# A two-block transformer forward pass on one core: norm statistics by token, eight slots of split weights, a first group of four units and a spare PSUM bank

## The chip, the core and the metric

The kernel runs on one core of a Trainium2 chip. Its engines are TensorE (PE in the rows), VectorE (DVE), ScalarE (ACT), GpSimd (POOL) and SyncE (SP). The metric is the device time of one execution in microseconds (us); the time of the kernel before is the median of three runs.

## The reference

Two blocks are computed one after the other on x of 512 tokens by 1024 features, in float32. Everything between the norms is a chain of products of an activation and a weight matrix:

```python
# first block: gmlp layer, feed-forward, banded attention layer, feed-forward
h = h + rms_norm(m, g[1])                       # m: gmlp or attention branch
f = jnp.square(jax.nn.relu(rms_norm(h, g[2]) @ w_up)) @ w_down
h = h + rms_norm(f, g[3])
# second block
h = h + 0.5 * swiglu(rms_norm_2(h, ffn1_norm), w_gate, w_up, w_down)
z = rms_norm_2(h, mix_norm) @ w_in              # top-k attention, retention, gates (rope by positions)
h = h + merged @ w_out
h = h + 0.5 * swiglu(rms_norm_2(h, ffn2_norm), ...)
h = h + sigmoid(rms_norm_2(h, ple_norm) @ w_ple_gate) * (p @ w_ple_proj)
return rms_norm_2(h, final_norm)
```

rms_norm divides by the root of the mean square of a token (plus 1e-6) and multiplies by a gain per feature.

## The kernel before

Activations lie feature-major: eight tiles of 128 features by 512 tokens (`DT` = 8). Precision comes from splitting: a value is written as a high part in the type float32r and a low part (the rest), and each product of a weight tile and an activation tile is three matmuls, high by high, high by low, low by high (`three_passes`, L368 to L370). Activations in split form are XH and XL, or HH and HL for the hidden layer.

The weights come as 411 **units**, numbered in the order in which TensorE uses them. A unit is 128 x 1024 float32 (some are narrower) and makes one PSUM bank of 128 x 512 from eight tiles, so from 24 matmuls. A unit is loaded by SP into RAW (4 slots), its high part is written to WH and its low part to WL (4 slots each): by ACT (`split_high`, L797) and DVE (`split_low`, L1128) in their instruction streams, just behind the work on the unit four places earlier, or by POOL (L316 and L319) in the ranges of `POOL_RANGES`. Those are units 0 to 19, 92 to 119 and 256 to 326. The semaphores count in unit order, so the first DVE split behind a POOL range waits until POOL has finished its last unit (`weights_split`), and the first ACT split likewise (`high_split`).

TensorE makes unit u in bank u mod 4 once its split is there and the unit before it in that bank is evacuated by DVE. Stages and their first units: gmlp_v 0, gmlp_u 8, gmlp_out 16, ffn_a0 24, att_v 88, att_kq 96, att_out 112, ffn_a1 120, ffn_b1 184, mix_heads 252, ret_qk 263, ret_v 271, ret_gate 279, merge 287, mix_out 319, ffn_b2 327, ple 395. A feed-forward takes groups: 8 units up (16 in the gated ones), then 8 units down, whose sums DVE adds into M; M is cleared by a memset at the start (L1229).

At a boundary between a branch and the next stage this happens. DVE copies the last bank into M, ACT squares it, DVE adds it to SS (`branch`, L1182 and L1140). `stat` (L460) multiplies SS by a matrix of ones, which gives each token's sum on all partitions; ACT takes the root into RI (L836), DVE the reciprocal of 128 x 512 (L1158). `post_and_pre` then goes over the eight tiles: z = M x RI (L1169), H updated (L1170), ACT squares H and writes XH, DVE writes XL (L1148). TensorE works on the first three units of the stage together, tile by tile as XL comes (`together`), with the second `stat` ahead of their last tile; the RI of that second norm is needed before the units can be evacuated (L1202, L1211). For token-major products `stat` also makes the sums with tokens on the partitions (L458, four matmuls of one column), and RT holds their reciprocal.

The rotation tables (sine and cosine, `rotation_tables`) are made on DVE and ACT during the last eight units of ffn_a1.

## Time and profile before

| | us |
|---|---|
| median of 3 runs (2697.91 to 2699.78) | 2698.27 |
| the profiled execution, its own time | 2702.41 |
| its span | 2700.6 |
| TensorE busy | 2487.4 |
| VectorE busy | 1434.4 |
| ScalarE busy | 796.1 |
| GpSimd busy | 518.7 |
| mean granted TensorE clock | 0.944 of full |

Matmuls are pipelined, so the busy time of TensorE counts overlaps as one; its idle time is what the boundaries between stages cost, and the clock column of a stretch shows whether its matmuls ran at 2.4 GHz (1.00) or at 1.2 GHz (0.50). DVE, ACT and POOL are busy for about half of the span or less, so they matter only where TensorE waits for one of them.

### The profile page before, as it was taken

To read this page: it belongs to the slowest core of one execution; us is meant where nothing else is said; L and a number is where in the kernel's file an instruction comes from. 1 tells how busy PE (TensorE), PEld (TensorE's weight loads), DVE (VectorE), ACT (ScalarE), POOL (GpSimd) and SP (SyncE) were. 2 spreads that over 40 slices of the span, in tenths; PEclk is the share of its full clock that TensorE was granted. 3 is DMA by queue.
4 is the path that set the end of the run, shared out by engine and by line. 5 is a ranking of instruction groups with operands and counts; after the bars stand their busy time and mean duration, and the time that the engine had idled before them with its cause. 6 is when DMAs were issued, how large, how long until landed. Compare 5 with 4: busy or idle time off the path is not lost.

```text
span 2700.6 us, 30486 instructions
## 1 busy us (share of the span) xinstructions
PE 2487.4 (92%) x10766; PEld 1964.8 (73%) x10766; DVE 1434.4 (53%) x1974; ACT 796.1 (29%) x1226; POOL 518.7 (19%) x243
## 2 busy tenths in 40 slices
PE   6888999979998999996999997978989998999996
PEld 5666888856666788884888885555567887888875
DVE  4566434473666543457534466797434336444456
ACT  2134223331433332233323232312322113322233
POOL 6600000015432000000000005452026871000000
PEclk9889999989998999997999998986599999999998
DMA  4222333322222233321333332121012323333322
GB/s 165 70 78 63 94 101 94 93 71 85 84 62 63 86 94 100 94 82 55 109 95 100 95 88 75 48 77 32 0 43 74 100 87 94 101 96 99 88 76 70
DMA packets 64805, 221.52 MB, mean 82 GB/s; under 512 B 7504, under 2 KB 9680, under 8 KB 64592
## 3 DMA queue, kind: packets, MB, share of 16 engines
q1 hardware_dynamic: 59184, 208.17, 26.0%
q10 hardware_dynamic: 5536, 12.19, 1.4%
q8 instruction: 56, 0.92, 0.1%
q14 instruction: 29, 0.24, 0.0%
HBM read 218.23 MB, written 2.10 MB: 82 GB/s over the span
## 4 chain that ended last, share of the span: by engine, by line
PE 81%; DVE 14%; ACT 2%; issue 2%; ACTq 0%; POOL 0%; DVEq 0%; POOLq 0%
PE PS L368 23%; PE PS L370 22%; PE PS L369 22%; PE PS L438 3%; DVE RI L1158 1%; PE PS L498 1%; PE PS L519 1%; DVE SS L1140 1%; DVE MK L1494 1%; DVE TOP L1493 1%; DVE XL L1148 1%; PE PS L708 1%; PE PS L625 1%; PE PS L646 1%; PE PS L635 1%
## 5 line engine op out<-in xcount | busy, mean ns | idle before, releaser
L368 PE MATMUL PS<-XH,WH 128*128 128x512 f32 x1816 | 730.3, 402 | 80.8 <-DVE WL L1128 35.6
L369 PE MATMUL PS<-XL,WH 128*128 128x512 f32 x1816 | 715.8, 394 | 0.0
L370 PE MATMUL PS<-XH,WL 128*128 128x512 f32 x1816 | 715.4, 394 | 0.0
L316 POOL TENSOR_TENSOR WH<-RAW,ONES 128x1024 fp32r<-128x1024 f32 (+1 forms) x119 | 231.0, 1942 | 1709.5 <-PE PS L370 1157.5
L368 PEld LDWEIGHTS PS<-XH,WH 128*128 128x128 f32 x1816 | 347.3, 191 | 182.4 <-issue 69.0
L1128 DVE TENSOR_TENSOR WL<-RAW,WH 128x1024 fp32r<-128x1024 f32 (+2 forms) x292 | 346.9, 1188 | 202.3 <-ACT WH L797 194.0
L370 PEld LDWEIGHTS PS<-XH,WL 128*128 128x128 f32 x1816 | 346.2, 191 | 73.9
L369 PEld LDWEIGHTS PS<-XL,WH 128*128 128x128 f32 x1816 | 347.3, 191 | 70.8 <-issue 1.4
L797 ACT ACTIVATE WH<-RAW 128x1024 fp32r<-128x1024 f32 (+2 forms) x292 | 297.8, 1020 | 340.2 <-DVE M L1240 336.2
L368 PE MATMUL PS<-HH,WH 128*128 128x512 f32 x992 | 389.6, 393 | 3.0 <-DVE WL L1128 3.0
L370 PE MATMUL PS<-HH,WL 128*128 128x512 f32 x992 | 386.8, 390 | 0.0
L369 PE MATMUL PS<-HL,WH 128*128 128x512 f32 x992 | 386.7, 390 | 0.0
L319 POOL TENSOR_TENSOR WL<-RAW,WH 128x1024 fp32r<-128x1024 f32 (+1 forms) x119 | 288.3, 2423 | 9.3
L368 PEld LDWEIGHTS PS<-HH,WH 128*128 128x128 f32 x992 | 186.5, 188 | 50.4 <-issue 9.1
L370 PEld LDWEIGHTS PS<-HH,WL 128*128 128x128 f32 x992 | 186.6, 188 | 39.0
L369 PEld LDWEIGHTS PS<-HL,WH 128*128 128x128 f32 x992 | 186.7, 188 | 38.0
L1240 DVE TENSOR_TENSOR M<-PS,M 128x512 f32 x80 | 55.2, 690 | 176.3 <-PE PS L370 176.0
L1195 DVE TENSOR_TENSOR HL<-T,HH 128x512 fp32r<-128x512 f32 (+1 forms) x108 | 74.8, 692 | 134.4 <-ACT HH L850 92.7
L438 PE MATMUL PS<-WH,XH 128*128 128x512 f32 x192 | 84.8, 442 | 60.2 <-DVE XL L1148 33.1
L847 ACT ACTIVATE T<-T 128x512 f32<-128x512 f32 x64 | 40.4, 632 | 200.3 <-DVE T L1202 200.3
L438 PEld LDWEIGHTS PS<-WH,XH 128*128 128x128 f32 x192 | 40.6, 211 | 73.7 <-issue 35.3
L1140 DVE TENSOR_TENSOR SS<-SS,T 128x512 f32<-128x512 f32 x91 | 76.1, 836 | 23.0 <-ACT T L803 23.0
(202 smaller groups left out, 2412.1 us busy)
## 6 DMA issues: line engine op xcount, KB each, us to landing
RAW<-in_weights SPq DMA_DIRECT2D x379, 512.0 KB, 3.5
RAW<-in_weights SPq DMA_DIRECT2D x16, 384.0 KB, 3.1
H<-in_xT ACTq DMA_DIRECT2D x8, 256.0 KB, 8.9
BIAS<-in_rel ACTq DMA_DIRECT2D x8, 256.0 KB, 3.5
RAW<-in_weights SPq DMA_DIRECT2D x8, 256.0 KB, 2.6
out<-R ACTq DMA_DIRECT2D x8, 256.0 KB, 2.2
BIAS<-in_rel ACTq DMA_DIRECT2D x8, 224.0 KB, 3.8
DECAY<-in_decay ACTq DMA_DIRECT2D x1, 1024.0 KB, 4.9
```

Source lines behind the costliest of these rows:

```text
L316: nc.gpsimd.tensor_tensor(WH[:, slot, 0:w], raw, ONES[:, 0:1].to_broadcast([P, w]), ALU.mult).then_inc(high_split, 1)
L319: nc.gpsimd.tensor_tensor(WL[:, slot, 0:w], raw, WH[:, slot, 0:w].bitcast(F32), ALU.subtract).then_inc(weights_split, 1)
L368: nc.tensor.matmul(PS[:, bank_, :], WH[:, slot, w], xh[:, k, :], start=(k == 0), stop=False)
L369: nc.tensor.matmul(PS[:, bank_, :], WH[:, slot, w], xl[:, k, :], start=False, stop=False)
L370: return nc.tensor.matmul(PS[:, bank_, :], WL[:, slot, w], xh[:, k, :], start=False, stop=stop)
L438: last = nc.tensor.matmul(PS[:, (first + j) % SLOTS, :], x[:, k, tok], wt[:, slot, w], start=(k == 0 and n == 0), stop=(k == DT - 1 and n ...
L797: S.activation(WH[:, slot, 0:w], RAW[:, slot, 0:w], ACT.Copy).then_inc(high_split, 1)
L847: S.activation(T[:, 1, :], T[:, 0, :], ACT.Square).then_inc(act_self, 1)
L1128: V.tensor_tensor(WL[:, slot, 0:w], RAW[:, slot, 0:w], WH[:, slot, 0:w].bitcast(F32), ALU.subtract).then_inc(weights_split, 1)
L1140: V.tensor_tensor(SS[:], SS[:], T[:, slot, :], ALU.add).then_inc(ss_ready, 1)
L1195: V.tensor_tensor(HL[:, f, :], T[:, src:src + 1, :], HH[:, f, :].bitcast(F32), ALU.subtract).then_inc(h_ready, 1)
L1240: V.tensor_tensor(M[:, f, :], PS[:, slot:slot + 1, :], M[:, f, :], ALU.add)\
```

## The change

Five things change, in one edit.

1. **Statistics by token.** `stat` now makes only the four one-column matmuls (into bank 6). ACT takes the root of 128 x 4, DVE its reciprocal into RT, and a new step `spread` on TensorE multiplies each reciprocal column, broadcast along the free axis, with the identity, which puts it on all partitions of a bank. After a branch, DVE reads that bank 4 directly; before a stage the bank is 5, and ACT copies it to RI.
2. **Eight slots.** In the ranges of `WIDE` (units 24 to 91, 120 to 255 and from 331 on) the split weights have eight slots instead of four, and ACT and DVE split unit u + 8 behind unit u (`AHEAD` = 8). RAW keeps four slots. The POOL ranges become units 0 to 27, 92 to 123 and 256 to 334.
3. **Four together, a fifth in bank 7.** A feed-forward starts with four units together; its fifth unit (28, 124, 188, 331) goes to bank 7 without waiting for an evacuation.
4. **No memset.** The first down group writes M instead of adding to it.
5. **Rotation tables later**, in the first down group of ffn_b1.

BIAS is loaded later in att_v, and several inner loops are written out. The core of the diff:

```diff
-POOL_RANGES = ((0, FIRST["gmlp_out"] + 4), (FIRST["att_v"] + 4, FIRST["ffn_a1"]),
-               (FIRST["mix_heads"] + 4, FIRST["ffn_b2"]))
+POOL_RANGES = ((0, 28), (92, 124), (256, 335))
+AHEAD = 8
+WIDE = ((24, 92, 20), (120, 256, 116), (331, UNITS, 328))
+SPARE = (28, 124, 188, 331)
+def weight_slot(u):
+    for first, end, zero in WIDE:
+        if first <= u < end:
+            return (u - zero) % (2 * SLOTS)
+    return u % SLOTS
+def slot_before(u):
+    return next((v for v in range(u - 1, max(-1, u - 3 * SLOTS), -1) if weight_slot(v) == weight_slot(u)
+                 and (weight_slot(u) < SLOTS or u - v == 2 * SLOTS)), None)
...
             def split_units(u, n, step=0):
-                    pool.wait_ge(units_done, u + s + 1 + step * SLOTS)
+                    if v == 24:
+                        pool.wait_ge(x_ready, 2 * DT)
+                    elif v == 120:
+                        pool.wait_ge(x_done, 2 * DT * TT)
+                    elif v == 332:
+                        pool.wait_ge(units_done, FIRST["mix_out"] + SLOTS)
+                    elif slot_before(v) is not None:
+                        pool.wait_ge(units_done, slot_before(v) + 1 + SLOTS + step * SLOTS)
...
+                if u in SPARE:
+                    bank.next()
+                else:
+                    pe.wait_ge(evacuated, bank.next())
...
-            def stat(token_major=False):
+            def stat():
                 pe.wait_ge(ss_ready, ss.next(DT))
-                if token_major:
-                    for j in range(TT):
-                        nc.tensor.matmul(PS[:, 5, j:j + 1], SS[:, j * P:j * P + P], ONES[:, 0:1],
-                                         start=True, stop=True)
-                nc.tensor.matmul(PS[:, 4, :], ONES[:], SS[:], start=True, stop=True).then_inc(stat_ready, 1)
+                for j in range(TT):
+                    last = nc.tensor.matmul(PS[:, 6, j:j + 1], SS[:, j * P:j * P + P], ONES[:, 0:1],
+                                            start=True, stop=True)
+                last.then_inc(stat_ready, 1)
+            def spread(bank_):
+                pe.wait_ge(ri_ready, ri.next())
+                for j in range(TT):
+                    last = nc.tensor.matmul(PS[:, bank_, j * P:j * P + P],
+                                            RT[:, TT + j:TT + j + 1].to_broadcast([P, P]), IDENT[:],
+                                            start=True, stop=True)
+                last.then_inc(spread_ready, 1)
...
                     if first:
-                        together(*[(DT, XH, XL, xr)] * 3, before_last=stat)
+                        together(*[(DT, XH, XL, xr)] * SLOTS, before_last=stat)
+                        spread(5)
...
+            def norm_rows():
+                root()
+                copy_rinv()
...
-            def rinv(token_major=False):
-                V.reciprocal(RI[:], RI[:]).then_inc(ri_ready, 1)
+            def rinv():
+                recip()
+                sp_.next()
+                dve.wait_ge(ri_copied, rc.next())
...
-                        link(V.tensor_tensor(z, m[:, t, :], RI[:], ALU.mult))
+                        link(V.tensor_tensor(z, m[:, t, :], PS[:, 4, :], ALU.mult))
...
-                    if tables and t < 5:
-                        rotation_tables(t)
-                    split_low(u + t + SLOTS)
+                    split_low(u + t + AHEAD)
...
-                V.memset(M[:], 0.0).then_inc(dve_self, 1)
-                dve.wait_ge(dve_self, me.next())
```

**VectorE in gmlp_out (units 16 to 23), from the evacuation of unit 16 on.** COPY M<-PS is one evacuation, WL<-RAW,WH one split. Before:

```order
L1182 COPY M<-PS 128x512 [waits units_done]
L1138 COPY SS<-T 128x512 [waits squares_ready]
L1128 TENSOR_TENSOR WL<-RAW,WH 128x1024 [waits weights_high_split,weights_split]
L1182 COPY M<-PS 128x512 [waits units_done]
L1140 TENSOR_TENSOR SS<-SS,T 128x512 [waits squares_ready,square_sum_ready]
L1128 TENSOR_TENSOR WL<-RAW,WH 128x1024 [waits weights_high_split]
```

Now, the same place from the evacuation of unit 19 on:

```order
L1267 COPY M<-PS 128x512 [waits units_done]
L1218 TENSOR_TENSOR SS<-SS,T 128x512 [waits squares_ready,square_sum_ready]
L1267 COPY M<-PS 128x512 [waits units_done]
L1218 TENSOR_TENSOR SS<-SS,T 128x512 [waits squares_ready,square_sum_ready]
L1206 TENSOR_TENSOR WL<-RAW,WH 128x1024 [waits weights_high_split,weights_split]
L1267 COPY M<-PS 128x512 [waits units_done]
L1218 TENSOR_TENSOR SS<-SS,T 128x512 [waits squares_ready,square_sum_ready]
L1206 TENSOR_TENSOR WL<-RAW,WH 128x1024 [waits weights_high_split]
```

The split that waits for POOL (`weights_split`) stood behind the first evacuation and stands now behind the fifth, with three evacuations queued behind it. att_out has the same order in both kernels' terms: before, its waiting split was already behind the fifth evacuation.

**GpSimd ahead of ffn_b2: the end of its last range.** WH_72 and WL_73 are the first four slots, WHA_77 and WL2_75 the new ones. Before, the last two units (325 and 326), each waiting for a unit of mix_out:

```order
L316 TENSOR_TENSOR WH_72<-RAW_71,ONES_103 128x1024 [waits units_done,weights_landed1]
L319 TENSOR_TENSOR WL_73<-RAW_71,WH_72 128x1024 [waits weights_high_split]
L316 TENSOR_TENSOR WH_72<-RAW_71,ONES_103 128x1024 [waits units_done,weights_landed2]
L319 TENSOR_TENSOR WL_73<-RAW_71,WH_72 128x1024 [waits weights_high_split]
```

Now, the last turn's unit 331 and the units 332 to 334 behind it:

```order
L362 TENSOR_TENSOR WH_72<-RAW_71,ONES_107 128x1024 [waits units_done]
L365 TENSOR_TENSOR WL_73<-RAW_71,WH_72 128x1024 [waits weights_high_split]
...
L362 TENSOR_TENSOR WHA_77<-RAW_71,ONES_107 128x1024 [waits units_done,weights_landed0]
L365 TENSOR_TENSOR WL2_75<-RAW_71,WHA_77 128x1024 [waits weights_high_split]
L362 TENSOR_TENSOR WHA_77<-RAW_71,ONES_107 128x1024 [waits weights_landed1]
L365 TENSOR_TENSOR WL2_75<-RAW_71,WHA_77 128x1024 [waits weights_high_split]
L362 TENSOR_TENSOR WHA_77<-RAW_71,ONES_107 128x1024 [waits weights_landed2]
L365 TENSOR_TENSOR WL2_75<-RAW_71,WHA_77 128x1024 [waits weights_high_split]
```

POOL takes eight units more, 327 to 334. Unit 331 has slot 3, which unit 327 holds, so it waits until TensorE has finished unit 327.

## Rows read from the trace of the kernel before

**Rows 1.** The page: the chain that ended last, by engine.
```profile
PE 81%; DVE 14%; ACT 2%; issue 2%; ACTq 0%; POOL 0%; DVEq 0%; POOLq 0%
```

**Rows 2.** Waits of PE: who for whom, total us, times, longest us.
```profile
PE PS L368 <- DVE WL L1128: 38.5, 10, 5.7
PE PS L368 <- DVE XL L1148: 26.7, 10, 8.4
```

**Rows 3.** Busy time by stretch: PE, PEld, DVE, ACT, POOL, clock, DMA share, GB/s.
```profile
260.00:540.00 280.00, 280.00 (x1237) 231.86 (x1236) 117.91 (x132) 84.83 (x104) 0.00 (x0) 1.00 0.33 97
236.80:241.90 5.10, 5.10 (x12) 4.04 (x13) 3.06 (x4) 2.51 (x4) 0.00 (x0) 0.50 0.35 103
204.50:207.80 3.30, 3.26 (x8) 2.62 (x9) 3.23 (x6) 1.41 (x3) 0.00 (x0) 0.50 0.00 0
```

**Rows 4.** Timeline at the start of ffn_a0: start, us, row [idle before <-releaser].
```profile
204.54 0.77 PE L368 MATMUL PS<-XH,WH 128*128 128x512 f32 x1 [8.15 <-DVE XL L1148]
...
224.31 3.35 DVE L1158 RECIPROCAL RI<-RI 128x512 f32<-128x512 f32 x1 [2.74 <-ACT RI L836]
...
228.58 3.47 DVE L1229 MEMSET M<- 128x4096 f32 x1 [0.92 <-DVE RI L1158]
...
232.43 0.69 DVE L1202 SCALAR_TENSOR_TENSOR T<-PS,RI 128x512 f32<-128x512 f32 x1 [0.38 <-DVE M L1229]
...
236.80 0.80 PE L368 MATMUL PS<-XH,WH 128*128 128x512 f32 x1 [5.72 <-DVE WL L1128]
```

**Rows 5.** Timeline: statistics by token, and four matmuls of 128 x 128.
```profile
42.37 0.95 PE L458 MATMUL PS<-ONES,SS 128*128 128x1 f32 x8
...
44.32 0.26 ACT L834 ACTIVATE RT<-PS,COL 128x4 f32<-128x4 f32 x1 [10.15 <-PE PS L460]
...
44.61 0.18 DVE L1155 RECIPROCAL RT<-RT 128x4 f32<-128x4 f32 x1 [9.89 <-ACT RT L834]
...
141.41 1.16 PE L553 MATMUL PS<-WST,VT 128*128 128x128 f32 x8 [1.34 <-DVE T L1351]
```

**Rows 6.** Timeline, DVE: the last SS of gmlp_out and the first z.
```profile
193.56 0.69 DVE L1140 TENSOR_TENSOR SS<-SS,T 128x512 f32<-128x512 f32 x1 [0.77 <-ACT T L803]
...
200.53 0.69 DVE L1169 TENSOR_TENSOR T<-M,RI 128x512 f32<-128x512 f32 x1
```

**Rows 7.** Timeline, POOL and DVE, in att_out.
```profile
825.20 1.89 POOL L316 TENSOR_TENSOR WH<-RAW,ONES 128x1024 fp32r<-128x1024 f32 x1 [25.53 <-PE PS L595]
...
841.90 2.40 POOL L319 TENSOR_TENSOR WL<-RAW,WH 128x1024 fp32r<-128x1024 f32 x1
...
844.34 1.22 DVE L1128 TENSOR_TENSOR WL<-RAW,WH 128x1024 fp32r<-128x1024 f32 x1 [4.27 <-POOL WL L319]
```

**Rows 8.** Timeline, POOL, DVE and PE, in mix_out and ffn_b2.
```profile
2232.95 2.34 POOL L316 TENSOR_TENSOR WH<-RAW,ONES 128x1024 fp32r<-128x1024 f32 x1
...
2235.37 2.73 POOL L319 TENSOR_TENSOR WL<-RAW,WH 128x1024 fp32r<-128x1024 f32 x1
...
2235.76 2.89 DVE L1148 SCALAR_TENSOR_TENSOR XL<-H,GAIN,XH 128x512 fp32r<-128x512 f32 x1
...
2276.70 0.79 PE L368 MATMUL PS<-XH,WH 128*128 128x512 f32 x1 [5.15 <-DVE WL L1128]
```

**Rows 9.** Timeline, PE: restarts at the other boundaries.
```profile
618.11 0.76 PE L438 MATMUL PS<-WH,XH 128*128 128x512 f32 x1 [4.41 <-POOL WL L319]
...
1217.41 0.50 PE L368 MATMUL PS<-HH,WH 128*128 128x512 f32 x1 [2.97 <-DVE WL L1128]
1236.92 2.07 PE L460 MATMUL PS<-SS,ONES 128*128 128x512 f32 x2 [6.75 <-DVE SS L1140]
...
1622.27 0.50 PE L368 MATMUL PS<-XH,WH 128*128 128x512 f32 x1 [2.55 <-DVE WL L1128]
...
2619.74 0.47 PE L368 MATMUL PS<-XH,WH 128*128 128x512 f32 x1 [3.43 <-DVE WL L1128]
...
2641.63 0.79 PE L368 MATMUL PS<-XH,WH 128*128 128x512 f32 x1 [5.52 <-DVE WL L1128]
```

More of the change, by code:

```diff
@@ L328, in _ @@
                     while u + same * SLOTS + SLOTS <= end and \
[L329 removed]
+                            widths[u + same * SLOTS:][:SLOTS] == widths[u:u + SLOTS] and \
+                            all(weight_slot(u + v) == v % SLOTS == (u + v) % SLOTS and
+                                slot_before(u + v) == u + v - SLOTS for v in range((same + 1) * SLOTS)):
                         same += 1
@@ L467, in group @@
                     if first:
-                        together(*[(DT, XH, XL, xr)] * 3, before_last=stat)
+                        together(*[(DT, XH, XL, xr)] * SLOTS, before_last=stat)
+                        spread(5)
+                    for s in range(SLOTS if first else 0, size * ups):
                         product(DT, XH, XL)
-                    with loop(pe, size * ups // 4 - first, [(split, 4), (bank, 4)]):
-                        for s in range(4):
-                            product(DT, XH, XL)
                     hr.next(size)
                     together(*[(size, HH, HL, hr)] * 2)
-                    for s in range(6):
+                    for s in range(DT - 2):
                         product(size, HH, HL)
-                per = 8 * ups + 8
+                per = DT * ups + DT
                 group(DT, first=True)
@@ L761, in _ @@
             together((DT, XH, XL, xr), (2, PTH, PTL, hr), (DT, XH, XL, xr), (2, PTH, PTL, hr), before_last=stat)
-            with loop(pe, 3, [(split, 4), (bank, 4)]):
-                for s in range(2):
-                    product(DT, XH, XL)
-                    product(2, PTH, PTL)
+            spread(5)
+            for s in range(6):
+                product(DT, XH, XL)
+                product(2, PTH, PTL)
             stat()
+            spread(5)
         @block.scalar
@@ new lines, in gated_units, with down_units @@
+                        split_low(u + 2 * s + 1 + AHEAD, turn)
+                def down_units(u, turn, added, tables=False):
+                    for s in range(DT):
+                        src = unit()
+                        if added:
+                            V.tensor_tensor(M[:, s, :], src, M[:, s, :], ALU.add).then_inc(evacuated, 1)
+                        else:
+                            V.tensor_copy(M[:, s, :], src).then_inc(evacuated, 1)
+                        if tables and s < 5:
+                            rotation_tables(s)
+                        split_low(u + s + AHEAD, turn)
@@ L1243, in ffn @@
+                up = gated_units if gated else plain_units
+                per = DT * ups + DT
+                up(first, DT, 0)
+                down_units(first + DT * ups, 0, False, tables)
+                with loop(dve, len(sizes) - 2, [(done, per), (ao, DT * ups)]) as o:
+                    up(first + per, DT, o * (per // SLOTS))
+                    down_units(first + per + DT * ups, o * (per // SLOTS), True)
                 u = first + per * (len(sizes) - 1)
```

294 lines of the change are left out of this document (148 added, 146 removed).

## The prediction

> **What bounds the kernel now.** I read the chain of waits first: 81% of it is TensorE, 14% DVE [rows 1]. So the time is TensorE's work plus the stretches in which it stands. The waits of TensorE name two releasers: a weight split on DVE, and the XL of a norm [rows 2]; both belong to the boundaries between stages. Inside ffn_a0, from 260 to 540 us, TensorE is busy all the time at full clock and issues 1237 matmuls in 280 us, 0.227 us each, so 5.44 us for a unit of 24 [rows 3]. Nothing in the change touches that rate. I go through the boundaries one by one; the price of each is the idle time in brackets in the timeline [rows 4, 9] and what the clock adds: after an idle stretch the granted clock is 0.50, that is 1.2 instead of 2.4 GHz, for 3.3 us at 204.5 and 5.1 us at 236.8 [rows 3], which costs half of the stretch.
>
> **The start of a feed-forward (four together, spare bank, eight slots, no memset).** In ffn_a0 the first matmul is at 204.54. Behind the second statistics stand the reciprocal (3.35 us from 224.31), the memset (3.47 us from 228.58), the first evacuation (232.43) and a split, and the fifth unit starts at 236.80 [rows 4]. Its successor, the sixth, would start 5.44 later plus 2.55 for the slow clock: 244.8. After: four units are 96 matmuls, 21.8 us, plus 0.95 for the statistics [rows 5] and 1.65 for the slow clock, end at 228.9. The eighth XL does not hold them: one tile takes DVE about 2.65 us, four units want 12 x 0.227 = 2.72. `spread` is four matmuls of 128 x 128 with a new weight each; the nearest row is 1.16 us [rows 5]. Its reciprocal is hidden behind the last tile. The fifth unit ends at 235.5. ACT's copy of RI (0.7) lets the first evacuation begin at 230.8; the second, one DVE period of 4.2 us later, ends at 235.7, and the sixth unit can go: gain 9.0. With the clock stretches of the other two stages the same sum gives 7.5 (ffn_a1) and 7.3 (ffn_b1). The memset becomes a write of the same size as the addition: nothing.
>
> **The statistics after a branch.** Before: last SS at 193.56, first z at 200.53, so 6.3 us between the end of the one and the start of the other [rows 6]. After: 0.95 + 0.26 + 0.18 + 1.16 from rows 5 and some 0.25 of hand-overs, 2.8 us at full clock. The two matmul pieces double at half clock: 4.9. I take 4.9 behind a long idle stretch, 3.7 elsewhere. The final norm also keeps ACT's copy: it gains 1.9.
>
> **The order of the splits in gmlp_out and att_out: a loss.** POOL alone needs 1.9 + 2.4 = 4.3 us a unit; with DVE at work between, 825.20 to 844.30 for four, 4.8 [rows 7]. In att_out before, DVE stood 4.27 us behind its fifth evacuation until POOL had finished unit 119 at 844.3 [rows 7]. Now POOL goes on to 123: 4 x 4.37 = 17.5 more, 861.8. DVE, in order, stands with three evacuations behind the waiting split, each 3.5 us with its square and split. The last SS, at 854.95 before, ends at 861.8 + 1.2 + 2 x 3.5 + 2.1 = 872.1: **17.1 later**. TensorE has finished unit 119 long before and has nothing else. In gmlp_out, POOL splits 20 to 27 instead of DVE; unit 20 can start when unit 16 is done, at 163.5. Eight units are 19.1 + 17.5 = 36.6, so 200.1; by the same tail the last SS ends at 210.45 instead of 194.25: **16.2 later**.
>
> At this place the Trainium skill has a rule against the change: "Perfetto Trace Analysis", on optimizing Scalar/DVE operations, says that moving work between DVE and GpSimd might not help, since they share a read port. The trace agrees: beside DVE a POOL unit takes 4.8 to 5.15 us instead of 4.3 [rows 7, 8]; rival 2 below is what the rule would make of the held units.
>
> **The start of ffn_b2: the third loss.** POOL now splits 327 to 334 too. In mix_out a POOL unit takes 5.15 us (2232.95 to 2238.10), and DVE's XL 2.89 [rows 8] instead of the 0.75 it has alone: the two take turns. Unit 326 is ready at 2238.1, so 327 to 330 at 2243.2, 2248.3, 2253.4 and, the end half alone, 2258.2. TensorE takes the first tile of all four units in turn, so it gets past the first tile only at 2258.2 (before: 2249.9, behind a DVE split). 87 matmuls, the statistics and a slow start: 19.7 + 1.0 + 2.3, four units at 2281.2. Unit 327 is done 2 us earlier, only then may POOL split 331: 2279.1 to 2283.5; the fifth unit ends at 2288.9. DVE has evacuated 327 and stands at its split of 335 until POOL has 334: 2279.1 + 17.5 = 2296.6, with the evacuation of 328 queued behind. Unit 332 needs that bank: it starts at 2298.6 and ends, slow clock included (2.5), at 2306.5. Before it ended at 2289.1 (fifth at 2276.70 [rows 8], two units, 1.5 for the clock): **17.4 later**.
>
> SBUF — State Buffer of the Trainium skill, "Who interferes with whom", says the pair shared by DVE and GpSimd is held for a whole instruction, and a DVE operation with two SBUF inputs counts. The XL of 2.89 us agrees [rows 8]. If they shared without blocking, POOL would keep 4.33 and 330 would be ready at 2255.4, and the sum would be 2.8 lower.
>
> **The other boundaries.**
> - att_v (618.11 [rows 9]): POOL splits 92 to 95 ahead, so it no longer slows DVE's eight tiles, which took 29 us and take 24 at 3.3 a tile. First matmul 2.2 earlier, 575.2; the first half ends 26.3 later, 601.5; spread, copy and four evacuations, 4.6. Second half at 606.1: gain 12.0.
> - ffn_a1, tables moved: TensorE stood 2.97 us with 1.7 of slow clock, and 6.75 us ahead of the statistics where 2.24 is the norm (the chain copy, square, sum) [rows 9]. Gain 2.97 + 1.7 + 4.5 = 9.1. In ffn_b1 the tables lie beside 8 down units: DVE's periods become 7.7, 5.6, 8.0, 5.6 and then 2, TensorE's is 5.44; the banks give four units of slack and the splits eight, the largest lag is 10 us, so hidden. If that cover fails, it costs up to the 9 it gave.
> - mix_heads: 2.55 [rows 9] less, and the first evacuation, which leads the following DVE-bound stretch, no longer waits for the long reciprocal: 4.0 in all.
> - ple: 3.43 + 0.46, then 5.52 [rows 9], a wait for a split: after, units in hand, it starts at once, its four end at 2630.2 and the next starts at 2632.8 instead of 2641.63: 8.8 and 1.6 of clock, 10.4.
> - gmlp_v: the spread and copy take the place of the reciprocal: nothing.
>
> **The sum.** gmlp_out to ffn_a0: +16.2 - 1.4 - 9.0 = +5.8. att_v: -12.0. att_out to ffn_a1: +17.1 - 0.7 - 7.5 = +8.9. ffn_a1 to ffn_b1: -9.1 - 2.4 - 7.3 = -18.8. mix_heads -4.0. ffn_b2 +17.4. ple -10.4. End -1.9. Together **-15.0**: the profiled execution of 2702.4 becomes 2687.4; the median of the runs is 4.1 below that execution, so 2683.3.
>
> Unknown prices: `spread` reads a broadcast column as its weights. Not less than the one-column pieces, 0.95, not more than a 512-wide sum at half clock, 2.1: ten of them, -2 to +9, I take 1.16. The sum of the slow-clock terms is uncertain by 8 either way, the entry of ffn_b2 by 5.
>
> **Rivals.**
> 1. The holds do not bind: POOL is ahead when DVE comes. Then 16.2 and 17.1 go, and ffn_b2 gains about 9 instead of losing 17.4: -60 more, 2623. For it: nothing in the change waits on purpose. Against: it needs under 2.7 us a unit, and the one hold there was before did bind [rows 7]. Chance 0.08.
> 2. Slower: the holds cost more than their length. Each leaves TensorE idle 8 to 17 us; if the clock then stays at 0.50 for some 14 us of work instead of 3 to 5, each of four restarts (one in gmlp_out, one in att_out, two at ffn_b2) costs 4.5 more, 18; and if DVE and POOL take turns in all twelve held units that I priced at 4.37, 12 x 0.78 = 9. Together +12: 2710. For: turns are what mix_out shows. Against: DVE itself stands during a hold, and 8 us idle ended with 3.3 us of slow clock [rows 3]. It decides from a slow stretch of 8 us on. Chance 0.11.
> 3. The holds as forecast, but the entries gain only the idle time and not the clock: 9 less, 2692. Chance 0.16.
> 4. The forecast, 2683: 0.65.
>
> A difference under 0.2% (5.4 us) is what a measurement can't tell from none. Rival 2 gives slower, 0.11; half of rival 3 with its spread, and the edge of the forecast's, give same, 0.11; the rest is faster, 0.78. The range: 2655, for larger clock gains and holds partly hidden, to 2703.
>
> **What would show it.** In att_out a DVE split behind the fifth evacuation with some 21 us of idle time released by POOL, and about as much in gmlp_out; at ffn_b2 a wait of TensorE for unit 328's evacuation of about 9 us and POOL active until about 17 us after unit 327. No idle time over 2 us at the fifth and sixth units of ffn_a0, ffn_a1 and ffn_b1. A z 3 to 5 us behind the last SS. Four rows of `spread` at about 1.2 us. ffn_a1 without waits before its last SS. The forecast is wrong if DVE's waits for POOL are short, or if TensorE stands at a place that isn't named here.

## The result: 0.5% faster, and the profile after

The changed kernel takes 2685.65 us (median of 5 runs, 2679.90 to 2688.23), the kernel before 2698.27 us beside it (5 runs): ratio 0.9947, 95% interval 0.9932 to 0.9962. The forecast was 2683. The profiled execution of the changed kernel took 2688.23 us, with a span of 2686.4.

The chain of the page, with POOL where it was nearly absent [rows 1]:
```profile
PE 80%; DVE 10%; POOL 4%; ACT 3%; issue 2%; DMA 0%; POOLq 0%; ACTq 0%; DVEq 0%
```
Waits of TensorE after (who for whom, total us, times, longest us):
```profile
PE PS L509 <- DVE SS L1218: 45.1, 5, 19.0
...
PE PS L420 <- DVE XL L1226: 12.3, 3, 4.1
PE PS L420 <- POOL WL L365: 9.8, 4, 4.1
PE PS L420 <- DVE T L1297: 9.1, 1, 9.1
```
The 38.5 us behind DVE's WL are gone, and XL fell from 26.7 to 12.3 [rows 2]. Three kinds of waits are new or longer: for two sums of squares TensorE now waits 18 and 19 us where it waited 2.2, then there are POOL's WL and one evacuation of 9.1 us. What is gone (53 us) and what is new (some 48 us) nearly cancel.

Inside a stage next to nothing changed. The second of the rows below has 1230 matmuls at clock 1.00 in the stretch where [rows 3] has 1237, and one small wait of 1.28 us, shown further down. The first is the restart of ffn_a0: 6.0 us at half clock, where it was 3.3 us behind the restart and 5.1 at the fifth unit. The columns are busy us and instructions of PE, PEld, DVE, ACT, POOL, then clock, DMA share, GB/s:
```profile
216.40:222.40 6.00, 5.97 (x14) 4.74 (x15) 5.89 (x10) 2.64 (x5) 0.00 (x0) 0.50 0.01 3
...
260.00:540.00 280.00, 278.72 (x1230) 230.44 (x1229) 119.89 (x135) 88.26 (x110) 0.00 (x0) 1.00 0.34 100
```
So I cut both traces at idle times of TensorE that exist in each of them. The table gives us per stretch, worked out from the ends of TensorE's work; the last three columns are kernels of the experiments, e1 without the holds in gmlp_out and att_out, e8 without all three and with three units together in ffn_b2, e9 with four slots and three units together:

| stretch ends with | before | after | difference | forecast | e1 | e8 | e9 |
|---|---|---|---|---|---|---|---|
| gmlp_out | 192.1 | 189.7 | -2.4 | 0 | 189.4 | 185.9 | 188.0 |
| ffn_a0 | 373.8 | 382.1 | +8.2 | +5.8 | 367.1 | 367.1 | 364.3 |
| att_v | 77.1 | 65.9 | -11.2 | -12.0 | 65.9 | 65.9 | 72.8 |
| att_out | 209.8 | 209.8 | 0 | 0 | 209.8 | 209.8 | 209.8 |
| ffn_a1 | 377.4 | 383.0 | +5.6 | +4.2 | 367.3 | 367.3 | 364.7 |
| ffn_b1 and the idle time in mix_heads | 435.7 | 414.7 | -21.0 | -18.1 | 413.5 | 413.4 | 418.0 |
| mix_out | 582.2 | 581.9 | -0.3 | 0 | 582.7 | 583.5 | 584.1 |
| the end | 452.5 | 459.3 | +6.8 | +5.1 | 458.9 | 435.3 | 447.9 |
| span | 2700.6 | 2686.4 | -14.2 | -15.0 | 2654.5 | 2628.3 | 2649.6 |

A stretch that an edit doesn't touch still differs by up to 3 us between kernels, the first by 4; smaller terms can't be read from it.

**The hold in gmlp_out.** A hold is the time for which DVE stands before a split that waits for POOL. DVE and TensorE (start, us, row, idle before and its releaser):
```profile
197.54 1.22 DVE L1206 TENSOR_TENSOR WL<-RAW,WH 128x1024 fp32r<-128x1024 f32 x1 [21.45 <-POOL WL L365]
...
207.06 0.69 DVE L1218 TENSOR_TENSOR SS<-SS,T 128x512 f32<-128x512 f32 x1 [0.77 <-ACT T L871]
...
212.42 0.69 DVE L1254 TENSOR_TENSOR T<-M,PS 128x512 f32<-128x512 f32 x1 [2.24 <-PE PS L518]
```
```profile
207.81 1.87 PE L509 MATMUL PS<-ONES,SS 128*128 128x1 f32 x8 [18.11 <-DVE SS L1218]
210.24 2.08 PE L518 MATMUL PS<-IDENT,RT 128*128 128x128 f32 x8 [0.56 <-DVE RT L1232]
216.43 0.77 PE L420 MATMUL PS<-XH,WH 128*128 128x512 f32 x1 [4.11 <-DVE XL L1226]
```
DVE stands 21.45 us before the split of unit 28, with three evacuations queued behind it; TensorE stands 18.1 us instead of 2.2. From the end of the last SS to the first z it is 4.7 us instead of 6.3 [rows 6], and both pieces of the statistics run at half clock. Between the last SS and TensorE's restart lie 8.7 us; before 10.3.

POOL meanwhile, undisturbed, 4.3 us a unit:
```profile
188.92 1.89 POOL L362 TENSOR_TENSOR WH<-RAW,ONES 128x1024 fp32r<-128x1024 f32 x1
190.89 2.34 POOL L365 TENSOR_TENSOR WL<-RAW,WH 128x1024 fp32r<-128x1024 f32 x1
193.19 1.89 POOL L362 TENSOR_TENSOR WH<-RAW,ONES 128x1024 fp32r<-128x1024 f32 x1
```

**The hold in att_out** [rows 7] is the same picture, once more 21.45 us:
```profile
856.21 1.22 DVE L1206 TENSOR_TENSOR WL<-RAW,WH 128x1024 fp32r<-128x1024 f32 x1 [21.45 <-POOL WLA L365]
```

**The start of ffn_a0** [rows 4]. No memset, and the fifth unit starts without a wait; but the first evacuation waits for ACT's copy of RI:
```profile
239.69 0.18 DVE L1232 RECIPROCAL RT<-RT 128x4 f32<-128x4 f32 x1 [6.26 <-ACT RT L898]
243.87 0.69 DVE L1285 SCALAR_TENSOR_TENSOR T<-PS,RI 128x512 f32<-128x512 f32 x1 [4.00 <-ACT RI L904]
```
A small wait is new, at the first down units of ffn_a0 and ffn_a1:
```profile
276.33 0.50 PE L420 MATMUL PS<-HH,WH 128*128 128x512 f32 x1 [1.28 <-DVE HL L1278]
```

**The start of ffn_b2** [rows 8]. TensorE after, then DVE:
```profile
2232.90 0.80 PE L420 MATMUL PS<-XH,WH 128*128 128x512 f32 x1 [4.08 <-POOL WL L365]
2237.95 0.80 PE L420 MATMUL PS<-XH,WH 128*128 128x512 f32 x1 [3.40 <-POOL WL L365]
...
2263.74 0.50 PE L420 MATMUL PS<-XH,WH 128*128 128x512 f32 x1 [1.49 <-POOL WL L365]
...
2278.56 0.76 PE L420 MATMUL PS<-XH,WHA 128*128 128x512 f32 x1 [9.08 <-DVE T L1297]
```
```profile
2276.59 1.22 DVE L1206 TENSOR_TENSOR WL<-RAW,WH 128x1024 fp32r<-128x1024 f32 x1 [12.92 <-POOL WL L365]
2277.73 0.68 DVE L1297 TENSOR_TENSOR T<-PS,RI 128x512 f32<-128x512 f32 x1
```
Unit 332 waits 9.1 us for the evacuation of 328, which stands behind the split that waits for POOL: the wait that the forecast named, of the length that it named.

### The profile page after: what moved, and what is told of

The parts are those of the page before. It is cut to its first block, busy times and chain, and to the rows that moved or that the text cites. A ratio compares the mean times of both kernels' runs of the same rounds, so it can differ in the third digit from the quotient of the medians.

```text
span 2686.4 us, 29675 instructions
## 1 busy us (share of the span) xinstructions
PE 2489.5 (93%) x10924; PEld 1980.5 (74%) x10924; DVE 1364.6 (51%) x1947; ACT 760.4 (28%) x1200; POOL 610.2 (23%) x283
## 4 chain that ended last, share of the span: by engine, by line
PE 80%; DVE 10%; POOL 4%; ACT 3%; issue 2%; DMA 0%; POOLq 0%; ACTq 0%; DVEq 0%
PE PS L420 23%; PE PS L422 22%; PE PS L421 22%; PE PS L489 3%; POOL WH L362 2%; POOL WL L365 2%; PE PS L563 1%; PE PS L584 1%; DVE WL L1206 1%; PE PS L774 1%; PE PS L690 1%; PE PS L711 1%; PE PS L700 1%; DVE MK L1574 1%; PE PS L573 1%
## 5 line engine op out<-in xcount | busy, mean ns | idle before, releaser
L420 PE MATMUL PS<-XH,WH 128*128 128x512 f32 x1792 | 714.6, 399 | 40.2 <-DVE T L1425 12.5
L421 PE MATMUL PS<-XL,WH 128*128 128x512 f32 x1792 | 703.7, 393 | 0.0
L422 PE MATMUL PS<-XH,WL 128*128 128x512 f32 x1784 | 700.4, 393 | 0.0
L362 POOL TENSOR_TENSOR WH<-RAW,ONES 128x1024 fp32r<-128x1024 f32 (+1 forms) x136 | 266.9, 1963 | 1654.8 <-PE PS L422 1530.3
L1206 DVE TENSOR_TENSOR WL<-RAW,WH 128x1024 fp32r<-128x1024 f32 (+2 forms) x272 | 322.4, 1185 | 248.4 <-ACT WH L865 192.2
L422 PE MATMUL PS<-HH,WL 128*128 128x512 f32 x992 | 386.3, 389 | 0.0
L865 ACT ACTIVATE WH<-RAW 128x1024 fp32r<-128x1024 f32 (+2 forms) x272 | 276.8, 1018 | 349.5 <-DVE M L1309 202.4
L365 POOL TENSOR_TENSOR WL<-RAW,WH 128x1024 fp32r<-128x1024 f32 (+1 forms) x132 | 322.5, 2443 | 10.4
L1278 DVE TENSOR_TENSOR HL<-T,HH 128x512 fp32r<-128x512 f32 x108 | 74.8, 692 | 127.2 <-ACT HH L928 92.7
L489 PE MATMUL PS<-WH,XH 128*128 128x512 f32 x192 | 82.3, 428 | 46.4 <-DVE XL L1226 22.4
L1309 DVE TENSOR_TENSOR M<-PS,M 128x512 f32<-128x512 f32 x48 | 33.1, 690 | 107.2 <-PE PS L422 106.8
L871 ACT ACTIVATE T<-H 128x512 f32<-128x512 f32 x72 | 45.4, 631 | 141.5 <-DVE H L1255 48.4
```

The source lines that it names most:

```text
L362: nc.gpsimd.tensor_tensor(high[:, 0:w], raw, ONES[:, 0:1].to_broadcast([P, w]), ALU.mult).then_inc(high_split, 1)
L365: nc.gpsimd.tensor_tensor(low[:, 0:w], raw, high[:, 0:w].bitcast(F32), ALU.subtract).then_inc(weights_split, 1)
L420: nc.tensor.matmul(PS[:, bank_, :], high[:, w], xh[:, k, :], start=(k == 0), stop=False)
L421: nc.tensor.matmul(PS[:, bank_, :], high[:, w], xl[:, k, :], start=False, stop=False)
L422: return nc.tensor.matmul(PS[:, bank_, :], low[:, w], xh[:, k, :], start=False, stop=stop)
L489: last = nc.tensor.matmul(PS[:, (first + j) % SLOTS, :], x[:, k, tok], wt[:, w], start=(k == 0 and n == 0), stop=(k == DT - 1 and n == 2))
```

## The experiments

All are edits of the changed kernel. Medians; each ratio is against the kernel before, timed beside it.

**1. The two holds taken away (e1_defer).**
```diff
+LATER = tuple(range(28, 32)) + tuple(range(124, 128))
...
 def branch(...):                      # ACT's branch_squares alike
-    split_low(u + t + AHEAD)
+    if u + t + AHEAD not in LATER:
+        split_low(u + t + AHEAD)
...
 def post_and_pre(..., later=None):    # ACT's pre_norm alike
     pre_tile(t - 1, gs)
+    if later and t > SLOTS:
+        split_low(later + t - SLOTS - 1)
```


> The changed kernel, with one thing moved: the eight splits of units 28 to 31 and 124 to 127, which DVE and ACT do in the last four steps of gmlp_out and att_out and the first of which waits until POOL has finished its range, are done in tiles 5 to 8 of the norm that follows. Theory (two holds): the last SS of gmlp_out was 15.9 us and that of att_out about as much later against the end of TensorE's stage than before the change; with the splits out of the way the two idle times of 18.1 and 19.0 us fall to 2 to 3 us, and the time is 30 to 38 us below the changed kernel, near 2652 us. Rival A (POOL itself is the limit: its WL of unit 27 ends at 197.5, so the first matmul of the feed-forward can't be earlier and waits for it): each place gives at most 5 us, 2676. Rival B (the time comes back, since the eight splits now lie beside the norm that TensorE waits for, at 2 x 0.7 us each): 5 us of the gain are lost, 2657.

Measured: 2654.46 us (5 runs), ratio 0.9833 (0.9821 to 0.9846), 31.2 below the changed kernel. The two stretches lose 14.9 and 15.7 us, the others next to nothing. TensorE at the same two places:
```profile
191.78 1.05 PE L511 MATMUL PS<-ONES,SS 128*128 128x1 f32 x8 [2.41 <-DVE SS L1223]
...
201.27 0.76 PE L422 MATMUL PS<-XH,WH 128*128 128x512 f32 x1 [5.84 <-DVE XL L1231]
```
```profile
835.70 1.87 PE L511 MATMUL PS<-ONES,SS 128*128 128x1 f32 x8 [3.51 <-DVE SS L1223]
```
POOL works as before (its WL of unit 27 ends at 198.2) and is not the limit; what cost was the place of the waiting split in DVE's queue. Rival B is there in small: the XL comes 1.7 us later than the 4.11 of the changed kernel. The holds are shown, and what the two give is 1.3 and 1.4 us under the forecast's 16.2 and 17.1.

**2. ffn_b2's start without POOL (e2_b2_split).**
```diff
-POOL_RANGES = ((0, 28), (92, 124), (256, 335))
+POOL_RANGES = ((0, 28), (92, 124), (256, 327))
+DUE = {319: (), ..., 323: (327,), 324: (328,), 325: (329,), 326: (330,),
+       327: (331, 332), 328: (333, 334), 329: (335, 336), 330: (337, 338)}
...
-split_low(u + 2 * s + AHEAD, turn)
+for v in DUE.get(u + 2 * s, (u + 2 * s + AHEAD,)):
+    split_low(v, turn)
```


> The changed kernel, with POOL's last range ended at 327 as before the change: ACT and DVE split units 327 to 330 in the last four steps of mix_out, and 331 to 338 two at a time behind the first four evacuations of ffn_b2; eight slots from 331 on and the spare bank stay. Theory (POOL's 4.3 to 5.1 us a unit sets the start of ffn_b2): the waits of TensorE for POOL's WL at 2228.8, 2234.6 and 2262.3 and the 9.1 us for the evacuation of 328 all go, and the DVE's XL take 0.75 instead of 2.9 us; 15 to 25 us less than the changed kernel, near 2667 us. Rival (the norm of mix_out and its reciprocal bound that place whoever splits): only the 9.1 us go, 2676.

Measured: 2670.45 us (4 runs), ratio 0.9903 (0.9888 to 0.9917), 15.2 below the changed kernel; the two profiled executions lie further apart, 19.6 us, of which 12.5 are in the last stretch (446.8 instead of 459.3), 4.0 in the first, which the edit doesn't touch, and the rest in small differences. The direction is shown, at the low end of the theory: the waits for POOL and the 9.1 us went, but three waits for DVE's WL took their place, the longest at the fifth unit:
```profile
PE PS L424 <- DVE WL L1213: 8.1, 3, 4.8
```

**3. Both (e3_both), and three together in ffn_b2 (e8_both_three).**
```diff
-together(*[(DT, XH, XL, xr)] * SLOTS, before_last=stat)
+together(*[(DT, XH, XL, xr)] * abreast, before_last=stat)   # 3 in ffn_b2, 4 elsewhere
```


> The changed kernel with both edits: the eight splits of gmlp_out and att_out done in the norm behind, and POOL's last range ended at 327 with the catch-up of the splits in ffn_b2. Theory (three separate holds, in three stretches that share nothing): the gains add, 31.2 and 15.2 us below the changed kernel's 2685.65: 2639. Rival (part of each gain came from the clock, which a later idle stretch takes back, or the two measured differences hold 4 us of their own spread each): 2645 to 2652.

> As e3_both, and in ffn_b2 alone the first three units go together instead of four. Theory (there the splits are late: with four together TensorE passes the first tile only after the split of unit 330, which DVE does behind the last tile; e2_b2_split and e5_four_slots show 32.5 us from the first idle time of that stage to the fifth unit, the kernel before with three together 28.6): 3 to 4 us less than e3_both. Rival (what is won at the first tile is lost at the fourth unit, which then waits for the same split): no difference, within 1.5 us.

Measured: e3 2644.5 us (6 runs, one of them 2683.5), ratio 0.9797 (0.9784 to 0.9809), 41.2 below the changed kernel and not 46.4: the rival with the spread of the two differences holds, at its lower edge. Part of experiment 2's difference was the first stretch, which e3 doesn't repeat (188.6 us for 185.7); the rest of the shortfall isn't taken apart. e8 2631.16 us (5 runs), ratio 0.9753 (0.9741 to 0.9766), 13.3 below e3 where I expected 3 to 4. The start of ffn_b2 in e3, TensorE:
```profile
2199.84 0.79 PE L426 MATMUL PS<-XH,WH 128*128 128x512 f32 x1 [1.44 <-DVE WL L1218]
2228.10 0.80 PE L426 MATMUL PS<-XH,WH 128*128 128x512 f32 x1 [4.83 <-DVE WL L1218]
```
and the stretch behind the second of them in e3, then the same place in e8, with the columns of the stretches above:
```profile
2228.00:2234.00 6.00, 5.90 (x14) 4.70 (x15) 4.93 (x7) 2.52 (x3) 0.00 (x0) 0.51 0.53 175
```
```profile
2194.80:2228.00 33.20, 33.20 (x154) 27.72 (x155) 13.02 (x16) 10.77 (x13) 0.00 (x0) 1.00 0.32 97
```
With three together both idle times go, and with them the half clock behind them, 3.4 and 5.8 us of work, worth half of that or 4.6: 1.44 + 4.83 + 4.6 = 10.9, against 11.1 measured from the start of ffn_b2 to the last statistics. I had seen the first idle time only. Four units together all end at one time, and only then is the slot free in which the fifth unit is to be split; with three together the first ends a unit's time earlier.

The splits of mix_out show the price of sharing in one kernel. DVE in e3, where POOL works without a break until it ends its range near 2186:
```profile
2180.97 0.68 DVE L1673 TENSOR_TENSOR H<-PS,H 128x512 f32<-128x512 f32 x1
2181.57 1.78 DVE L1230 TENSOR_TENSOR SS<-SS,T 128x512 f32<-128x512 f32 x1
2183.27 2.89 DVE L1238 SCALAR_TENSOR_TENSOR XL<-H,GAIN,XH 128x512 fp32r<-128x512 f32 x1
2186.08 0.68 DVE L1673 TENSOR_TENSOR H<-PS,H 128x512 f32<-128x512 f32 x1
2186.68 0.68 DVE L1230 TENSOR_TENSOR SS<-SS,T 128x512 f32<-128x512 f32 x1
2187.28 0.74 DVE L1238 SCALAR_TENSOR_TENSOR XL<-H,GAIN,XH 128x512 fp32r<-128x512 f32 x1
```
The same XL takes 2.89 us beside POOL and 0.74 without, the sum of squares 1.78 and 0.68; the evacuation, which has one input in PSUM, takes 0.68 either way.

**4. Without the spare bank (e4_no_spare).**
```diff
-SPARE = (28, 124, 188, 331)
+SPARE = ()
```


> The changed kernel without the spare bank: the fifth unit of each feed-forward writes the bank of the first and waits for its evacuation. Theory, from the changed kernel's trace: the first evacuation of ffn_a0 ends at 244.6, and the fifth unit began at 243.5, since the four together and the slow clock fill the time until then; so the bank is worth about 1 us at each of three starts and nothing in ffn_b2: 2 to 5 us more, near 2689. Rival (the bank carries the entry's gain, as the prediction had it with a fifth unit that ends five us before the evacuation is there): 5 us at each of three starts and more by the clock, 2703 or more.

Measured: two kinds of runs. Four of 12 took 2685.4 to 2689.2, which is the theory; eight took 2719.8 to 2725.7, and the median is 2720.67 us. The ratio, which mixes both kinds, is 1.0036 (1.0000 to 1.0072). In the profiled one, of the longer kind, ffn_a0 and ffn_a1 take 381.3 and 381.7 us, no more than with the bank, though the fifth unit now waits 1.6 us for its bank: what the spare bank gives is less than what a stretch differs by itself. What is longer lies in mix_heads: from TensorE's restart there to its next idle time the same work takes 139.9 us instead of 97.9. The granted clock is at half for 109 us instead of 13.7, and 97.6 of them are work, where it was 3.8. A stretch of it, first in the changed kernel and then here:
```profile
1700.00:1725.00 25.00, 25.00 (x87) 14.86 (x86) 18.59 (x23) 9.67 (x16) 11.80 (x6) 1.00 0.14 43
```
```profile
1693.00:1718.00 25.00, 25.00 (x40) 10.49 (x40) 8.80 (x12) 6.30 (x12) 4.51 (x3) 0.50 0.07 21
```
TensorE is never idle in either; it issues 40 matmuls instead of 87. The kernel's higher median is thus not a wait for the bank; it comes by the clock. No execution of the shorter kind was traced.

**5. Four slots (e5_four_slots), and with three together (e9_four_slots_three).**
```diff
-POOL_RANGES = ((0, 28), (92, 124), (256, 335))
-AHEAD = 8
-WIDE = ((24, 92, 20), (120, 256, 116), (331, UNITS, 328))
-SPARE = (28, 124, 188, 331)
+POOL_RANGES = ((0, 20), (92, 120), (256, 327))
+AHEAD = 4
+WIDE = ()
+SPARE = ()
...
-together(*[(DT, XH, XL, xr)] * SLOTS, before_last=stat)   # e9 alone
+together(*[(DT, XH, XL, xr)] * 3, before_last=stat)
```


> The changed kernel with the split weights as before the change: four slots, splits four ahead, POOL's ranges 0 to 20, 92 to 120 and 256 to 327, no spare bank. What stays is the statistics by token, the first four units together, no memset, the tables in ffn_b1. Theory (the eight slots as they are filled cost more than they give: +16, +17 and +17 us at three holds against some 12, 10 and a few us at att_v, ple and the fifth units): near 2656 us, about 30 less than the changed kernel. Rival (the slots pay for themselves, and the gain of the change is theirs): not below 2683. It also tells the terms of the other parts: before minus this is what they give together, forecast as about 42 us.

> e5_four_slots (four slots, splits four ahead, no spare bank) with the first three units of each feed-forward together, as before the change, instead of four. Theory (four together need eight slots: with four, the four units end at one time, and only then can the slot of the first be split again, so the fifth unit waited 4.8 to 5.1 us at each of four starts and met the half clock for 3.4 to 6.8 us; with three together the first unit ends a unit's time earlier): 12 to 25 us less than e5_four_slots, near 2656 us. Rival (the idle time only moves one unit on, as in the kernel before the change): within 4 us of 2673.7.

Measured: e5 2673.68 us (4 runs), ratio 0.9902 (0.9888 to 0.9917); e9 2651.43 us (5 runs), ratio 0.9824 (0.9810 to 0.9837). The four slots are 12 us faster than the eight, not 30; my estimate had missed what four together cost when there are four slots. ffn_a0 of e5:
```profile
228.26 0.79 PE L420 MATMUL PS<-XH,WH 128*128 128x512 f32 x1 [5.09 <-DVE WL L1206]
```
In e9 that wait isn't there, at none of the four starts. The four stretches with these starts are 6.0, 4.3, 6.7 and 10.3 us shorter than in e5, together 27.3 of the 27.5 us between the two profiled executions. So the parts other than slots, bank and four together give 46 us of the kernel before (2697.9 to 2651.4); the forecast's terms for them, with four together counted in, had come to about 42. And against e8, four slots lose 6.9 us in att_v, 4.6 in ffn_b1 and 12.6 in the last stretch, all of it in ple (ffn_b2 takes 361.7 us in both), and win 2.8 and 2.6 in ffn_a0 and ffn_a1. In these last two e8 also starts four units together and has the splits of experiment 1 in the norm, so what is won there isn't the slots' alone.

**6. The tables back in ffn_a1 (e6_tables_back).**
```diff
 def branch(u, added, m=M, shift=0, tables=False):
     add_square(t == 0)
+    if tables and t < 5:
+        rotation_tables(t)
...
-ffn(FIRST["ffn_b1"], FFN_B, True, ..., tables=True)
+ffn(FIRST["ffn_b1"], FFN_B, True, ...)
```


> The changed kernel with the rotation tables back in ffn_a1's last eight down units. Theory (the prediction's term): TensorE stands 2.97 us there, 4.5 us more ahead of the statistics, and 1.7 us go to the clock: 9 us more, 2695. Rival A (the tables are not free in ffn_b1 either: DVE is behind at its first down group): 4 to 6 us more, 2691. Rival B (with splits eight ahead the work of the tables is hidden in ffn_a1 too, since DVE may be eight units behind): at most 3 us more, 2688.

Measured: 2692.32 us (11 runs), ratio 0.9981 (0.9972 to 0.9990), 6.7 above the changed kernel. The stretch behind ffn_a1, in which the delay shows (ffn_b1's in the table), takes 423.9 us instead of 414.7, 9.2 more, where the forecast had 9.1; TensorE waits
```profile
1236.48 1.87 PE L509 MATMUL PS<-ONES,SS 128*128 128x1 f32 x8 [11.61 <-DVE SS L1221]
```
instead of 2.24. That is one wait where the forecast had three pieces (2.97 of standing, 4.5 ahead of the statistics, 1.7 of clock), presumably since with splits eight ahead DVE's delay shows only at the end; the sum is the same. Rival B falls; A's number fits the total, but its reason isn't seen in the trace: the rest are differences in stretches that the edit doesn't touch.

**7. The old statistics (e7_old_stats).**
```diff
 def stat(token_major=False):
...
-    last.then_inc(stat_ready, 1)
+    nc.tensor.matmul(PS[:, 4, :], ONES[:], SS[:], start=True, stop=True).then_inc(stat_ready, 1)
...
-V.reciprocal(RT[:, TT:2 * TT], RT[:, 0:TT]).then_inc(ri_ready, 1)   # and spread, copy_rinv
+V.reciprocal(RI[:], RI[:]).then_inc(ri_ready, 1)
```


> The changed kernel with the statistics as before the change: a 512-wide sum on TensorE, a 512-wide root on ACT and the long reciprocal on DVE, no spread, no copy. Theory, from the changed kernel's trace: a branch's z begins 4.7 us behind the last SS instead of 6.3, so 1.6 us at gmlp_out and about 2.6 at two others (6.8); at the entries root, reciprocal, spread and copy take 4.5 us from the sums to the first evacuation, and root and long reciprocal about as long, so nothing there; 0.9 at each half of gmlp_v and att_v and 1.3 at the end: about 10 us more, 2695. Rival (the prediction's use of it: at the entries the long reciprocal is 3 us later on the path to the sixth unit, four times): 2708.

Measured: 2694.42 us (11 runs), ratio 0.9983 (0.9975 to 0.9992), 8.8 above the changed kernel: the theory, not the rival. In ffn_a0 the long reciprocal even lets the first evacuation begin sooner, 25.8 us behind TensorE's restart (216.84 to 242.59) where it is 27.4 with reciprocal, spread and copy (216.43 to 243.87):
```profile
239.20 3.35 DVE L1203 RECIPROCAL RI<-RI 128x512 f32<-128x512 f32 x1 [5.32 <-ACT RI L881]
242.59 0.69 DVE L1245 SCALAR_TENSOR_TENSOR T<-PS,RI 128x512 f32<-128x512 f32 x1
```
That stretch is 382.0 us with the old statistics and 382.1 with the new. The statistics by token give 2.2 us at att_v, 2.6 in ffn_b1's stretch, and 2.3 from the last statistics to the end.

**8. TensorE kept at work in the idle times of mix_heads (e10_fill from e8, e11_no_spare_fill from e4).** The added matmuls compute nothing that is used.
```diff
+def idle_work(bank_, n):
+    for m in range(n):
+        nc.tensor.matmul(PS[:, bank_, :], XH[:, m % DT, 0:P], XH[:, m % DT, :],
+                         start=(m == 0), stop=(m == n - 1))
...
+idle_work(6, 52)
 pe.wait_ge(evacuated, v_ready)
```


> e8_both_three with TensorE kept at work in the two long idle times of mix_heads (14.0 and 15.2 us in its trace): 52 matmuls of 128x512 into a bank that nobody reads, put in front of each. Theory (the 17.1 us at half clock behind each idle time come from the idling, and cost work that is needed): both low stretches go, 5 to 8 us less for the first, up to as much for the second, 2631 becomes 2617 to 2626. Rival A (what follows is bound by DVE, so TensorE's clock there is free): within 2 us of 2631. Rival B (the added matmuls run late and hold up the transposes): slower, up to 2640.

> e4_no_spare with the same 52 matmuls in the first idle time of mix_heads. e4_no_spare had two kinds of runs, four of 2685 to 2689 and eight of 2720 to 2726, and the profiled one of the longer kind stayed at half clock for 109 us behind that idle time instead of 13.7. Theory (the longer kind is this one stretch of clock): with TensorE at work there all runs are of the short kind and somewhat below it, 2676 to 2684. Rival (the clock stays low for another reason, say the thin work of the index scores behind): both kinds remain, or 2720 stays the median.

Measured: e10 2631.54 us (5 runs), ratio 0.9754 (0.9741 to 0.9767), the same as e8. That is the number of rival A, but not its reason. The two stretches at half clock fell from 17.1 and 17.1 us to 6.8 and 3.4, yet what went was mostly the idle time in them: behind the restarts TensorE worked at half clock for 6.8 and 5.0 us in e8 and still for 6.7 and 3.4 in e10. So little was there to win. Nor is TensorE's clock free at this place. From the first restart to the next idle time TensorE is busy throughout, and it takes 97.9 us in e3, with 3.6 us of it at half clock, and 99.3 in e8, with 6.8: the 3.2 us more at half clock cost 1.4.

e11 2724.57 us (4 runs, all of the longer kind), ratio 1.0098 (1.0082 to 1.0113): my theory falls. Three stretches of its trace:
```profile
1640.00:1655.00 15.00, 13.38 (x60) 10.74 (x58) 13.50 (x11) 5.04 (x8) 12.45 (x5) 1.00 0.32 99
1655.00:1680.00 25.00, 24.05 (x56) 13.76 (x57) 11.85 (x20) 7.89 (x18) 4.24 (x2) 0.55 0.07 21
...
1700.00:1750.00 50.00, 50.00 (x75) 19.60 (x74) 15.70 (x21) 11.00 (x20) 6.51 (x4) 0.50 0.07 21
```
TensorE was at work at full clock until 1655, with one idle time of 2.3 us, and the clock fell all the same and stayed low through the index scores, for 95.6 us. In e10 the same idle time of 2.3 us was followed by 6.7 us. What decides is open. It isn't the long idle time ahead. By the count of runs it goes with the edit: 12 of 16 runs of e4 and e11 are of the longer kind and one of 66 of all the others from the changed kernel on, a run of e3 (2683.5 us, mean clock 0.937 where the other five have 0.952 to 0.954, not traced). But e5 and e9, which have no spare bank either, show it in none of nine.

**9. No stage held by POOL (e12_catch_up).**
```diff
-POOL_RANGES = ((0, 28), (92, 124), (256, 335))
+POOL_RANGES = ((0, 20), (92, 120), (256, 327))
+DUE = {u: (u + SLOTS,) for first in (gmlp_out, att_out, mix_out) for u in range(first, first + DT)}
+for first in (24, 120, 327):
+    DUE.update({first + n: (first + 4 + 2 * n, first + 5 + 2 * n) for n in range(SLOTS)})
...
+for v in due(u + s):
+    split_low(v, turn)
...
-together(*[(DT, XH, XL, xr)] * SLOTS, before_last=stat)
+together(*[(DT, XH, XL, xr)] * 3, before_last=stat)
```


> The changed kernel with no stage held by POOL: its ranges end at 20, 120 and 327 as before the change (it still starts at 92), DVE and ACT split four ahead in gmlp_out, att_out and mix_out, and catch up to eight ahead by splitting two units behind each of the first four evacuations of the feed-forward that follows; three units together everywhere, spare bank and eight slots kept. Theory (e8_both_three takes 367.1 and 367.3 us from the end of gmlp_out to the end of ffn_a0 and from the end of att_out to the end of ffn_a1, e9_four_slots_three without POOL there 364.3 and 364.7, and from there on e8_both_three is the faster): 2631.2 less 5.4, near 2626 us. Rival (two splits behind an evacuation make DVE late at the fifth unit of ffn_a0 and ffn_a1, whose plain units leave DVE less room than the gated ones): idle time of TensorE there, 2631 or more.

Measured: 2631.27 us (5 runs), ratio 0.9752 (0.9738 to 0.9765), the same as e8. ffn_a0 and ffn_a1 take 365.5 and 365.9 us, some 1.5 less each than in e8, without a wait at the fifth unit, so the rival's reason isn't there. The 5.4 us were not had: 3 came, and att_out (211.4), ffn_b1 (414.9) and the first stretch took them back. e8 and e12 are the fastest kernels here, 2.5% below the one before and 2.0% below the changed one (2631.2 to 2685.65).

## Why the prediction was right

The total, its sign and its mechanism came out, 2683 for 2685.65: gains at the boundaries, most of them eaten by three holds. The gain of the entries came out smaller, and ffn_b2's term was right as the sum of two wrong parts. Step by step:

- **The holds in gmlp_out and att_out**, +16.2 and +17.1: right. DVE's wait for POOL is 21.45 us in both (I had asked for some 21), and experiment 1 takes 14.9 and 15.7 us out. Against the end of TensorE's work the last SS of gmlp_out came 15.9 us later than before (2.2 and 18.1 us). That e1 wins a little less is the XL, 1.7 us later there.
- **The hold in ffn_b2**, +17.4: ffn_b2 grew from 367.5 to 386.3 us, +18.8. The steps are where the forecast had them: unit 332 starts 51.5 us behind the end of mix_out, forecast 50.5. But the same sum had ffn_b2 gain 9 us once the hold is gone (rival 1), so it put the hold at 26. Experiments 2 and 3 have 372.6 and 372.8 us there, 13.6 less than with the hold and still 5 more than before the change: without POOL, four together wait for the slot of the first. Only with three together does it come to 361.7, 5.8 less than before.
- **ple and the end**, -10.4 and -1.9: from the end of ffn_b2 on it is 73.1 us instead of 85.0, -11.9.
- **The entries**, -9.0, -7.5 and -7.3: the mis-sized term, and for a reason that I had wrong. From TensorE's restart to the start of ffn_a0's sixth unit it was 40.25 us (204.54 to 244.8) and is 32.5 (216.43 to 248.93), so -7.75, and 1.3 of that is given back at the first down unit. Half clock after the restart lasted 6.0 us, not 3.3. For ffn_a1 the stretch leaves some 5.6 of the 7.5, once the hold, the statistics and the tables are taken out; ffn_b1's entry I can't separate. And I put the gain on the whole bundle; the runs show that its parts stand in for each other. With eight slots, taking away the spare bank alone (e4) or the short reciprocal alone (e7) costs nothing there; with four slots and three together (e9) ffn_a0 is faster still, 364.3.
- **The statistics after a branch**: -1.4 forecast in gmlp_out, 10.3 to 8.7 us measured between the last SS and the restart, -1.6. At the places where I had taken 3.7 us for the new chain and not 4.9 (-2.2 within att_v's term, -2.4 ahead of ffn_b1), both pieces ran at half clock too, 1.87 and 2.08 us, and 1.80 and 2.08, and from the statistics to the restart it gave 0.7 and 1.7 us. `spread` itself takes 1.05 us at full clock and 2.08 at half; I had 1.16.
- **The tables**: 9.1 forecast, 9.2 measured in their stretch by experiment 6; the cover in ffn_b1 holds.
- **att_v**: -12.0 forecast, -11.2 measured. The first matmul came 0.3 us earlier and not 2.2, and the pause before the second half is 3.6 us and not 4.6. e9, with four slots, has 6.9 less of it.
- **The first stretch**, 0 forecast, -2.4 measured. The 512-wide sum is gone from its middle, but it differs by up to 4 us between kernels, so I can't tell.
- **Rival 1** (the holds don't bind) falls with the 21.45 us. **Rival 2**: its condition, half clock for some 14 us of work behind a hold, didn't come; it was 6.0 in ffn_a0. Its other half, that DVE and POOL take turns in all held units, didn't either: POOL's unit in the hold takes 4.3 us, for DVE itself stands. SBUF — State Buffer of the Trainium skill, "Who interferes with whom", says that a DVE instruction with two SBUF inputs contends with a GpSimd instruction that reads SBUF, and one with at most one SBUF input, outside the two-port modes, does not; the XL of 2.89 us and the evacuation of 0.68 in experiment 3 agree. **Rival 3** would give 2692; the traces don't show it, since the stretch of half clock at the fifth unit (6.8 us in each of ffn_a0, ffn_a1 and ffn_b1 before, part of it idle) is gone at all three. What the clock took back is the longer half clock behind the restart of ffn_a0.

The errors, -2.4, +2.4, +0.8, +1.4, -2.9, -0.3 and +1.7 by stretch, add up to under 1 us. That is luck in part: most of them are larger than their sum, and in ffn_b2 a hold put 13 us too high and a start put 14 us too fast cancelled within one term.

## What to carry over

A split that waits for a slower engine, put in the queue ahead of evacuations, can cost most of the time for which it waits, here 15 and 16 of 21.45 us; move the wait behind the work that others need before changing who does the work. Buffers, a spare bank and a shorter operation that all shorten one wait are not to be added up: take them one at a time, since here the plain version with four slots and three units together was 34 us faster than the bundle. And units that run together end together, which frees their slots at the worst time.
